# The last four tiles of an output projection computed as two halves of 256 tokens, each half in a PSUM bank of its own

## The reference, cut to what matters

```
h = x + 0.5 * swiglu(rmsnorm(x, ffn1_norm[l]), ...)
u = rmsnorm(h, mix_norm[l]);  p = u @ w_in[l]
ret = retention(...);  dif = diff_attn(...)
h = h + concat([ret, dif]) @ w_out[l]          # the output projection
h = h + 0.5 * swiglu(rmsnorm(h, ffn2_norm[l]), ffn2_wg[l], ffn2_wu[l], ffn2_wd[l])
x = rmsnorm(h, final_norm[l])
```

## Time and profile before

| | |
|---|---|
| median of 3 runs | 2061.37 us (2058.81 to 2061.59) |
| span of the profiled execution, first to last instruction | 2056.0 us |
| median less span | 5.4 us |
| PE busy | 95% of the span |
| weight loads (PEld) busy | 78% |
| DVE, ACT, POOL busy | 46%, 32%, 42% |

### The profile page before, as it was taken

One profiled execution on the slowest core, in us unless ns is written; L12 is line 12 of the kernel. 1 busy time (PEld: TensorE's weight loads), 2 busy tenths in 40 slices (PEclk: granted clock), 3 DMA queues, 4 the chain that ended last, 5 costly groups with the idle time before them and its releaser, 6 DMA issues.

```text
span 2056.0 us, 25133 instructions
## 1 busy us (share of the span) xinstructions
PE 1961.8 (95%) x8630; PEld 1604.5 (78%) x8630; DVE 951.3 (46%) x1095; ACT 647.8 (32%) x909; POOL 873.4 (42%) x392
## 2 busy tenths in 40 slices
PE   7949999999899899999999999999988999999997
PEld 5838888887688788888878888888867878888886
DVE  5412454426856541532554245443386655334145
ACT  4112222435533321222342222224454332222124
POOL 4324444444343444444444444444433335444442
PEclk9979999999999999999999999999999999999999
DMA  4332222232111222322223222323211123322222
GB/s 142 97 100 100 98 97 96 88 103 72 48 65 62 94 101 92 102 92 92 82 86 130 99 95 93 100 78 108 92 52 62 52 82 102 102 92 94 100 90 74
DMA packets 54094, 185.51 MB, mean 90 GB/s; under 512 B 6356, under 2 KB 7636, under 8 KB 54020
## 3 DMA queue, kind: packets, MB, share of 16 engines
q1 hardware_dynamic: 53172, 182.26, 26.8%
q10 hardware_dynamic: 720, 2.10, 0.3%
q0 software_dynamic: 128, 0.20, 0.0%
HBM read 181.39 MB, written 3.15 MB: 90 GB/s over the span
## 4 chain that ended last, share of the span: by engine, by line
PE 79%; DVE 9%; issue 8%; ACT 2%; POOL 2%; DVEq 0%; POOLq 0%; ACTq 0%
PE bank L438 18%; PE bank L439 18%; PE bank L440 18%; PE pair L440 7%; PE pair L438 7%; PE pair L439 7%; POOL w_lo L396 2%; DVE a_hi L952 1%; DVE neg_max L1097 1%; PE pair L619 1%; PE bank L634 1%; ACT s L847 1%; DVE acc L918 1%; ACT hg_hi L735 1%; DVE hg_lo L907 1%
## 5 line engine op out<-in xcount | busy, mean ns | idle before, releaser
L396 POOL TENSOR_TENSOR w_lo<-raw,w_hi 128x1024 fp32r<-128x1024 f32 (+1 forms) x344 | 825.3, 2400 | 1130.1 <-ACT w_hi L690 1130.0
L690 ACT ACTIVATE w_hi<-raw 128x1024 fp32r<-128x1024 f32 (+1 forms) x344 | 355.3, 1034 | 717.8 <-PE bank L440 514.3
L438 PE MATMUL bank<-hg_hi,w_hi 128*128 128x512 f32 x1120 | 441.9, 395 | 0.0
L439 PE MATMUL bank<-hg_lo,w_hi 128*128 128x512 f32 x1120 | 437.4, 391 | 0.0
L440 PE MATMUL bank<-hg_hi,w_lo 128*128 128x512 f32 x1120 | 437.2, 390 | 0.0
L438 PE MATMUL bank<-a_hi,w_hi 128*128 128x512 f32 x768 | 301.7, 393 | 31.8 <-POOL w_lo L396 27.4
L439 PE MATMUL bank<-a_lo,w_hi 128*128 128x512 f32 x768 | 299.4, 390 | 0.0
L440 PE MATMUL bank<-a_hi,w_lo 128*128 128x512 f32 x768 | 299.3, 390 | 0.0
L438 PE MATMUL pair<-hg_hi,w_hi 128*128 128x512 f32 x704 | 275.5, 391 | 0.0
L440 PE MATMUL pair<-hg_hi,w_lo 128*128 128x512 f32 x704 | 273.9, 389 | 0.0
L439 PE MATMUL pair<-hg_lo,w_hi 128*128 128x512 f32 x704 | 273.9, 389 | 0.0
(11 more groups left out here) (176 smaller groups left out, 1544.8 us busy)
## 6 DMA issues: line engine op xcount, KB each, us to landing
raw<-in_w_gu SPq DMA_DIRECT2D x176, 512.0 KB, 3.2
raw<-in_w_dn SPq DMA_DIRECT2D x64, 512.0 KB, 3.2
raw<-in_w_p SPq DMA_DIRECT2D x56, 512.0 KB, 3.2
raw<-in_w_dn SPq DMA_DIRECT2D x32, 384.0 KB, 3.0
raw<-in_w_o SPq DMA_DIRECT2D x16, 512.0 KB, 3.2
h<-in_x ACTq DMA_DIRECT2D x4, 512.0 KB, 9.8
out_y<-h SPq DMA_DIRECT2D x8, 256.0 KB, 2.2
cs<-in_cossin SPq DMA_DIRECT2D x2, 512.0 KB, 4.2
```

Of the source, the lines that this page charges most:

```text
L396: pool.tensor_tensor(w_lo[:, s, 0:tiles, :].rearrange("p a b -> p (a b)"), raw[:, s % RAW, 0:n], w_hi[:, s, 0:tiles, :].rearrange("p a b - ...
L438: pe.matmul(out, w_hi[:, s, k, :], m_hi, start=first, stop=False)
L439: pe.matmul(out, w_hi[:, s, k, :], m_lo, start=False, stop=False)
L690: act.activation(w_hi[:, s, 0:tiles, :].rearrange("p a b -> p (a b)"), raw[:, s % RAW, 0:tiles * P], ACT.Copy).then_inc(hi_done, 1)
```

## The change

Tiles 4 to 7 are computed as two halves of 256 tokens, one after the other. Half 0 of a tile goes to the left half of one bank, half 1 to the right half of another: tiles 4 and 6 use banks 0 and 1, tiles 5 and 7 banks 4 and 5. Each half is 24 matmuls of 128x256, in the order high-high, low-high, high-low for every k, so `w_lo` is waited for at the start of a tile. VectorE adds each half as soon as it is done. Tile 4 needs two banks free and so waits for add 1 where it waited for add 0; tile 5 waits for add 3 where it waited for add 1; tile 6 for add 4 and tile 7 for add 5. The next block's first product waits for add 6.

```diff
         out_done = signal("out_done", KD * (2 * len(CHUNKS) + 1))
+        half_done = signal("half_done", KD - 4)
+        def half_bank(o, b):
+            return out_banks[2 * (o % 2) + b][:, b * SEQ:(b + 1) * SEQ]
...
-                                    pe.wait_ge(h_ready, at(h_ready, l, KD + len(CHUNKS) * KD + 6))
+                                    pe.wait_ge(h_ready, at(h_ready, l, KD + len(CHUNKS) * KD + 7))
...
                 for o in range(4, KD):
-                    pe.wait_ge(h_ready, at(h_ready, l, KD + len(CHUNKS) * KD + o - 3))
-                    last = fresh_product(l, out_banks[o % 4], U_OUT + o, o % SLOTS, a_hi, a_lo)
-                    last.then_inc(out_done, 1)
+                    pe.wait_ge(h_ready, at(h_ready, l, KD + len(CHUNKS) * KD + (2, 4, 5, 6)[o - 4]))
+                    pe.wait_ge(lo_done, at(lo_done, l, U_OUT + o + 1 + RAW))
+                    for b in range(BATCHES):
+                        cols = slice(b * SEQ, (b + 1) * SEQ)
+                        for k in range(KD):
+                            last = three(half_bank(o, b), (o % SLOTS, k), a_hi[:, k, cols], a_lo[:, k, cols], k == 0,
+                                         k == KD - 1)
+                        last.then_inc(out_done if b else half_done, 1)
...
-                    add_output(l, len(CHUNKS) * KD + k, k, out_banks[k % 4], 1.0)
+                    if k < 4:
+                        add_output(l, len(CHUNKS) * KD + k, k, out_banks[k], 1.0)
+                    else:
+                        dve.wait_ge(half_done, at(half_done, l, k - 3))
+                        dve.tensor_tensor(h[:, k, 0:SEQ], half_bank(k, 0), h[:, k, 0:SEQ], ALU.add)
+                        dve.wait_ge(out_done, at(out_done, l, len(CHUNKS) * KD + k + 1))
+                        dve.tensor_tensor(h[:, k, SEQ:T], half_bank(k, 1), h[:, k, SEQ:T], ALU.add).then_inc(h_ready, 1)
```

## The result

| | before | after |
|---|---|---|
| median (20 runs each) | 2059.99 us (2057.14 to 2061.59) | 2063.63 us (2061.55 to 2065.27) |
| ratio | 1 | 1.0017, 95% interval 1.0011 to 1.0024 |
| span of the profiled execution | 2056.0 us | 2063.4 us |

The change costs 3.6 us, against a forecast of 3.15. That is under the 0.2% that was to count as a change, so "no change" is what was predicted and what came; with 20 runs each the interval shows it as a small loss all the same.

The account below looks back on a forecast made before the run. The prediction took VectorE's lateness, which makes TensorE stand, as the cause of the loss. Layer 0's +1.05 us and layer 1's +2.10 summed to +3.15, or 2064.5 us; range 2061 to 2073.

Parts of the forecast that it names:

- The bound: Output projection: VectorE's lateness makes TensorE stand, losing 8.46 and 7.37 us; after the change TensorE bounds from tile 5.
- Adds 0 to 3 keep their times: VectorE's adds of the untouched tiles 0 to 3 stay put; in layer 0 add 3 ends at 664.29.
- Stand before tile 4: TensorE stands 5.2 us before tile 4 for add 1; the wait for `w_lo` costs nothing.
- The price of a short matmul: Tiles 4 to 7: a 128x256 matmul costs 0.1065 + 0.0135 = 0.120 us; bounds 0.111 and 0.216.
- Rivals 1 and 2: Tiles 4 to 7: dearer matmul, +4.3 to +11.8 us, chance 0.20; weight load paces it, +23 us, chance 0.08.
- Loads and matmuls overlap: Weight loads stay hidden behind the 0.120 us matmuls; the contrary row-group rule would give +54 us, chance 0.01.
- The clock: Tile 4 runs 6.7 us at 0.50 and takes 8.7 us, hidden behind add 3 to within 0.1 us.
- Rival 3: Clock falls late, in tiles 5 and 6 instead of tile 4: 3.3 us a layer, +9.8 us in all, chance 0.12.
- Tile 5 to 7 and the product: Tiles 5 to 7 run without a stand from 664.35; next block's first product starts at 681.63, not waiting for `hg_lo`.
- Adds by halves: VectorE's half adds take 0.43 us each; only one follows tile 7's last matmul, off TensorE's path.
- The sum: Mean-square matmul later by 1.05 us in layer 0 and 2.10 in layer 1, together +3.15 us.
- Rival 4: Faster: the wait for add 3 before tile 5 does not bind, -3.6 and -2.5 us, 2055 us, chance 0.04.

Follow-up runs that it names:

- e5: Kernel before with VectorE's adds one tile ahead and ScalarE's splits for the next block's units 2 and 3 behind `hg_hi` 7: 2043.25 us, ratio 0.9922.
- e7: Kernel before with tiles 4 to 7 as 96 matmuls of 128x128, four quarters in the tile's old bank: 2127.84, 2168.91 and 2170.34 us.
- e4: Changed kernel with VectorE's two half adds of tile k + 1 placed before `hg_lo` of tile k: 2050.75 us, ratio 0.9957 to the kernel before.
- e6: Changed kernel with VectorE's adds one tile ahead and ScalarE's later splits for units 2 and 3: 2050.24 us, ratio 0.9955 to the kernel before.
- e3: Kernel before with only VectorE's order changed, add of tile k + 1 before `hg_lo` and `acc` of tile k: 2054.96 us, ratio 0.9980.
- e1: Kernel before with tiles 4 to 7 as 48 matmuls of 128x256, both halves in the old bank, add waits unchanged: 2057.88 us, ratio 0.9988.

## Why the prediction was right

By its own steps, with times from add 0 on:

- **The bound.** VectorE's late chain, then TensorE from tile 5 on. Shown by e5 (the loss of before goes with the lateness and the two meetings) and by the stands of the changed kernel.
- **Adds 0 to 3 keep their times.** 6.46 and 15.12 us after add 0, against 6.54 and 15.21.
- **Stand before tile 4.** 5.2 us forecast, 5.26 measured. `w_lo` cost nothing there.
- **The price of a short matmul.** 0.120 us forecast from the two clock levels of the long one, 0.120 measured. Rivals 1 and 2 of the prediction, a dearer matmul and a load that paces it, both fall. The way to it was in part lucky. The prediction says that 0.0135 us do not depend on the level of the clock, but takes all of the 0.426 at the lower level as streaming; with a cost that is the same at both levels the same two rows would have given 0.127. The changed kernel shows the 0.0135 at full clock only (0.213 at the lower level, half of 0.426). And e7 shows that the formula stops holding somewhere between 256 and 128 columns: at 128 it gives 0.067, where 0.111 came, the pace of line 609.
- **Loads and matmuls overlap.** The row of a weight load still says 189 ns while pairs are 120 ns apart, and 0.1065 us of the 0.120 are streaming by the rows of the lower clock, which leaves 0.0135 for a load that overlaps nothing. So the rule of the Trainium skill (page "TensorE: Matmul & The Clock Gate", Part 3, "The mechanism") that a load overlaps only a matmul of another row group does not hold here, where every load goes to all rows.
- **The clock.** It was hidden, as forecast, but the prediction put all of its 6.7 us into tile 4. It was down about that long, from near 654.2 to 660.9 us, but the first 2.9 of it lay in the stand before the tile. Tile 4 took 7.6 us in place of 8.7 and was over early enough for a stand of 0.93 us (0.58 in layer 1) where I had none. This stand costs nothing, since add 3 ends it; the sum had tile 4 end within 0.1 us of add 3, so an error of this size the other way would have cost about 1 us a layer. Rival 3 needed the full clock through tile 4; it did not come.
- **Tile 5 to 7 and the product.** The first product starts 33.30 us after add 0, forecast 33.23; no wait for `hg_lo`; mean-square matmul at 44.21 and 44.20, forecast 44.11 and 44.10. The 0.1 us is in the start of tile 5, 0.81 us after add 3's start where I had 0.74.
- **Adds by halves.** 0.42 us, forecast 0.43. No gain from the first half, since the last one alone releases `h_ready`.
- **The sum.** +3.15 forecast, +3.35 in the seams, +3.6 in the medians (2.3 to 4.9 by the interval). The rest between the last two is within the scatter of the untouched parts.

Rival 4 needed an earlier add 3. e4 and e6, where add 3 comes 8.4 us after add 0 in place of 15.1, show that it would indeed have been faster, but only by an order that the change does not have.

What failed was outside the prediction: I expected e3 to give 9 to 15.8 us, because I left GpSimd to the rival: two meetings of `hg_lo` with its subtractions and, in one layer, the lower clock took most of the gain. GpSimd's subtractions follow ScalarE's splits, and these follow the adds, so a new order on VectorE moves them too.

## What to carry to other kernels

When TensorE stands at a seam, ask first who is late and what that engine meets on its way; splitting TensorE's tiles gave it more work and freed nothing, while an order of VectorE and ScalarE that hides one wait and avoids two meetings with GpSimd gave 16 us, of which the hidden wait alone gave 4. When a version's times fall into two groups, a median between them describes neither (e1): look at the granted clock of each execution. Two banks for one tile mean that the tile waits for the later of two adds: price that wait before the matmuls. Sum over a seam from one event in the profile to another rather than over the span, whose other parts scattered here by more than the effect.

## What the runs showed of the hardware

- A matmul in this format with its own weight load costs 0.2267 us for 512 columns (rows 5), 0.120 for 256 (after) and 0.111 for 128 (e7) at full clock, and 0.426, 0.213 and 0.213 at a granted clock of 0.50. Below 256 columns next to nothing is gained.
- With 128 columns the clock went to 0.50 and stayed there for four tiles of back-to-back matmuls, 82 us, in the execution profiled (e7, 2170.34 us); another of the three took 42.5 us less.
- The same two stands of TensorE (0.72 and 2.62 us) cost 2.57 us more in the layer in which the clock fell with them (e3, 40.96 against 38.39).
- VectorE's `hg_lo`, with two operands from SBUF, takes 0.74 us alone and up to 2.83 beside a subtraction of GpSimd (e3), ending 0.55 us after it; its adds from PSUM took 0.68 or 0.69 in every row shown.
